# Folding a norm gain into the weight split, reordering the first loads, and starting the first product on half the tokens

## The reference

```python
def rms_norm(x, g):
    y = x * lax.rsqrt(jnp.mean(x * x, axis=-1, keepdims=True) + RMS_EPS)
    return y * g

h = rms_norm(x, norm1_g)          # x: (1, 512, 1024), norm1_g: (1024,)
proj = h @ w_in                   # w_in: (1024, 2816)
qa, ka, va, qb, kb, vb, gb = jnp.split(proj, ...)
...
```

## Time and profile before

| | us |
|---|---|
| time of the kernel before, median of 3 runs (601.34 to 603.32) | 601.63 |
| time of the profiled execution | 602.76 |
| its span in the profile | 601.0 |
| TensorE busy | 570.4 (95%) |
| VectorE busy | 422.0 (70%) |
| ScalarE busy | 350.4 (58%) |
| GpSimd busy | 133.9 (22%) |
| first pass of a product (block 0) starts at | 24.42 |
| last pass of block 0 hands over to block 1 at | 35.33 |

### The profile page before, as it was taken

One profiled execution on the slowest core, in us unless ns is written; L12 is line 12 of the kernel. 1 busy time (PEld: TensorE's weight loads), 2 busy tenths in 40 slices (PEclk: granted clock), 3 DMA queues, 4 the chain that ended last, 5 costly groups with the idle time before them and its releaser, 6 DMA issues.

```text
span 601.0 us, 8110 instructions
## 1 busy us (share of the span) xinstructions
PE 570.4 (95%) x2791; PEld 465.9 (78%) x2792; DVE 422.0 (70%) x559; ACT 350.4 (58%) x458; POOL 133.9 (22%) x116
## 2 busy tenths in 40 slices
PE   4899999999999999997999999999999999999973
PEld 3788878888877888876788888888888888888851
DVE  3812565554673854275489989889989889989867
ACT  4723435583133433340678778878778878778623
POOL 4320000000000000015503443233444233411170
PEclk9999999999999999998999999999999999999997
DMA  8996222202220236896399999999999999993163
GB/s 300 380 368 211 70 71 71 70 1 71 70 71 0 71 106 247 280 369 225 94 336 360 376 382 372 371 371 366 372 384 379 373 373 371 360 387 120 43 258 140
DMA packets 72141, 144.85 MB, mean 241 GB/s; under 512 B 3907, under 2 KB 13291, under 8 KB 71985
## 3 DMA queue, kind: packets, MB, share of 16 engines
q1 hardware_dynamic: 65936, 125.49, 59.1%
q0 software_dynamic: 6176, 19.00, 9.0%
HBM read 132.89 MB, written 14.71 MB: 246 GB/s over the span
## 4 chain that ended last, share of the span: by engine, by line
PE 83%; DVE 7%; DMA 4%; issue 2%; ACT 2%; SPq 1%; POOL 1%; POOLq 0%; DVEq 0%; ACTq 0%
PE ps L1226 23%; PE ps L1228 22%; PE ps L1227 22%; PE ps L1233 5%; DMA arena<-w_in 2%; PE ps L1298 2%; PE ps L1268 2%; PE ps L1241 2%; PE ps L1335 1%; PE ps L1323 1%; DMA arena<-y_dram 1%; PE ps L1289 1%; PE ps L1362 1%; DVE res L1187 1%; DVE act_lo L836 1%
## 5 line engine op out<-in xcount | busy, mean ns | idle before, releaser
L1026 DVE TENSOR_TENSOR lo_ring<-arena,hi_ring 128x2048 fp32r<-128x2048 f32 x94 | 215.2, 2292 | 37.6 <-ACT hi_ring L741 36.6
L1226 PE MATMUL ps<-hi_ring,act_hi 128*128 128x512 f32 x576 | 232.2, 403 | 1.2 <-DVE act_lo L836 1.2
L1228 PE MATMUL ps<-hi_ring,act_lo 128*128 128x512 f32 x576 | 225.2, 391 | 0.0
L1227 PE MATMUL ps<-lo_ring,act_hi 128*128 128x512 f32 x576 | 224.7, 390 | 0.0
L741 ACT ACTIVATE hi_ring<-arena 128x2048 fp32r<-128x2048 f32 x94 | 180.1, 1917 | 20.8 <-PE ps L1228 20.8
L1226 PEld LDWEIGHTS ps<-hi_ring,act_hi 128*128 128x128 f32 x576 | 108.4, 188 | 28.2 <-issue 6.0
L1228 PEld LDWEIGHTS ps<-hi_ring,act_lo 128*128 128x128 f32 x576 | 108.3, 188 | 23.6
L1227 PEld LDWEIGHTS ps<-lo_ring,act_hi 128*128 128x128 f32 x576 | 108.5, 188 | 20.5
L827 DVE TENSOR_TENSOR lo_ring<-arena,hi_ring 128x512 fp32r<-128x512 f32 x68 | 45.0, 688 | 43.3 <-ACT hi_ring L615 42.8
L539 POOL DMA_INDIRECT y_dram<-y,row_info x15 | 16.1, 1072 | 154.8 <-issue 154.8
L836 DVE TENSOR_TENSOR act_lo<-ps,act_hi 128x512 fp32r<-128x512 f32 x64 | 41.6, 683 | 11.0 <-ACT act_hi L779 4.9
(11 more groups left out here) (179 smaller groups left out, 546.7 us busy)
## 6 DMA issues: line engine op xcount, KB each, us to landing
arena<-w_gate SPq DMA_DIRECT2D x32, 1024.0 KB, 11.9
arena<-w_up SPq DMA_DIRECT2D x32, 1024.0 KB, 11.7
arena<-w_down SPq DMA_DIRECT2D x32, 1024.0 KB, 12.0
arena<-w_in SPq DMA_DIRECT2D x16, 512.0 KB, 9.4
y_dram<-arena POOLq DMA_DIRECT2D x8, 512.0 KB, 11.2
arena<-w_out SPq DMA_DIRECT2D x4, 1024.0 KB, 5.1
arena<-y_dram SPq DMA_DIRECT2D x8, 512.0 KB, 6.8
arena<-w_in SPq DMA_DIRECT2D x3, 1024.0 KB, 15.8
```

The lines of the kernel that those rows point to most:

```text
L1026: nc.vector.tensor_tensor(lo(N1 + n12), raw(n12), hi(N1 + n12).bitcast(F32), ALU.subtract).then_inc(lo_done, 1)
L1226: nc.tensor.matmul(dst, a_hi, b_hi, start=start, stop=False)
L1227: nc.tensor.matmul(dst, a_hi, b_lo, start=False, stop=False)
L1228: return nc.tensor.matmul(dst, a_lo, b_hi, start=False, stop=stop)
```

## The change

It has four parts.

1. **The gain.** `norm1` only multiplies x by the reciprocal root, with a TENSOR_SCALAR. The gain comes as 8 columns of 128 values (`gain1_col`, in the buffer `over`), fetched by GpSimd's first DMA in runs of one 4-byte element. In the split of blocks 0 to 10 ScalarE's copy has the gain column as its scale, and VectorE's subtraction becomes a SCALAR_TENSOR_TENSOR (raw times gain minus high). For blocks 0 and 1 that is two instructions for each piece on VectorE, for block 2 two on both engines, for blocks 3 to 10 one.
2. **The loads.** SyncE issues x 0, the identity alone (64 KB), x 1, weight block 0, x 2, x 3, weight block 1, the rest of `keep`, and then blocks 2 to 14. GpSimd issues five of its loads only when x 3 has landed.
3. **The start.** There are four `h_buf`, and tile t has bank 4+t for its transposes: first for its first four blocks of 128 (half 0), later, when the low part of these is written, for the other four (half 1). Block 0 is multiplied in two passes over the tokens: tiles 0 and 1 (256 columns), then tiles 2 and 3. The squares go to SBUF (`hi_ring`) instead of PSUM. The fills are 2, 10 and 10.
4. **The order.** ScalarE and VectorE mix the splits of block 0 into the work on the tiles; the splits of blocks 1 and 2 come behind all of it. `STEPS` starts with block 1.

```diff
-START_FILL = (2, 4, 6, 2, 12)
+START_FILL = (2, 10, 10)
...
-STEPS = [(g, t) for g in range(N1 - 2) for t in range(T)] + [(g, t) for t in range(T) for g in (N1 - 2, N1 - 1)]
+STEPS = [(g, t) for g in range(1, N1 - 2) for t in range(T)] + [(g, t) for t in range(T) for g in (N1 - 2, N1 - 1)]
...
-        h_buf = [region(O_P, D), region(O_PT, D)]
-        gain1 = region(O_QKB, D)
+        h_buf = [region(o, D) for o in (O_P, O_PT, O_QKB, O_QKB + D)]
+        gain1_col = over[:, T * N_LOGITS:T * N_LOGITS + KD].bitcast(F32)
...
+            load_x(0)
+            sp.dma_start(ident, table[:, C_IDENT:C_IDENT + P]).then_inc(ident_in, 16)
+            load_x(1)
+            load1(0)
+            load_x(2)
+            load_x(3)
+            load1(1)
+            sp.dma_start(keep[:, P:C_KEEP], table[:, P:C_KEEP]).then_inc(keep_in, 16)
+            for g in range(2, N1):
                 load1(g)
...
+            pool.dma_start(gain1_col, bass.AP(norm1_g.tensor, 0, [[1, P], [P, KD]]), allow_slow_non_contiguous=True
+                           ).then_inc(gain1_in, 16)
...
+            pool.wait_ge(x_in[T - 1], 16)
+            pool.dma_start(sinks[:, :], bass.AP(attn_sinks.tensor, 0, [[0, P], [1, 8]])).then_inc(sinks_in, 16)
...
             pool.wait_ge(rel_copied, 1)
...
-                nc.scalar.activation(dst, src, ACT.Copy).then_inc(hi_done, 1)
+                for cols, gain in gains(g, piece):
+                    if gain is None:
+                        ins = nc.scalar.activation(dst, src, ACT.Copy)
+                    elif g == 2:
+                        ins = nc.scalar.activation(dst[:, cols], src[:, cols], ACT.Copy, scale=gain)
+                    else:
+                        ins = nc.scalar.activation(dst, src, ACT.Copy, scale=gain)
+                ins.then_inc(hi_done, 1)
...
+            square_x(0)
+            square_x(1)
+            turned_hi(0, 0)
+            split_piece(0, 0)
+            turned_hi(1, 0)
+            split_piece(0, 1)
+            square_x(2)
+            square_x(3)
+            split_piece(0, 2)
+            turned_hi(2, 0)
+            split_piece(0, 3)
+            turned_hi(3, 0)
             for t in range(T):
+                turned_hi(t, 1)
             for piece in range(4):
                 split_piece(1, piece)
+            for piece in range(4):
+                split_piece(2, piece)
...
-                nc.vector.tensor_tensor(dst, src, src_hi.bitcast(F32), ALU.subtract).then_inc(lo_done, 1)
...
+                    elif g < 2:
+                        for a in range(2):
+                            ins = nc.vector.scalar_tensor_tensor(dst[:, :, a, :], src[:, :, a, :], gain,
+                                                                 src_hi[:, :, a, :].bitcast(F32), ALU.mult, ALU.subtract)
+                    else:
+                        ins = nc.vector.scalar_tensor_tensor(dst, src, gain, src_hi.bitcast(F32), ALU.mult, ALU.subtract)
...
-                nc.vector.scalar_tensor_tensor(h_buf[t % 2], res_t[:, t, :], rms[:, t:t + 1], gain1,
-                                               ALU.mult, ALU.mult).then_inc(h_ready, 1)
+                nc.vector.tensor_scalar(h_buf[t], res_t[:, t, :], rms[:, t:t + 1], None, ALU.mult).then_inc(h_ready, 1)
...
+            def first_block(half, k):
+                tok = slice(half * 2 * P, (half + 1) * 2 * P)
+                w_hi, w_lo = (as_chunks(v)[:, k, :] for v in (hi(0), lo(0)))
+                pe.wait_ge(lo_done, k + 1)
+                for t in range(T):
+                    cols = slice(t * P, (t + 1) * P)
+                    ins = triple(ps[:, t, tok], w_hi[:, cols], w_lo[:, cols], ht_hi[:, k, tok], ht_lo[:, k, tok],
+                                 half == 0 and k == 0, False)
+                    if half and k == 3:
+                        ins.then_inc(mm_done, 1)
...
+            fill(START_FILL[0])
+            turn_h(0, 0)
+            fill(START_FILL[1])
+            turn_h(1, 0)
...
+            fill(START_FILL[2])
+            pe.wait_ge(h_lo, 2)
+            first_block(0, 0)
+            first_block(0, 1)
...
+            turn_h(2, 0)
+            turn_h(3, 0)
+            first_block(0, 2)
+            first_block(0, 3)
+            turn_h(0, 1)
+            turn_h(1, 1)
+            pe.wait_ge(h_lo, T)
+            first_block(1, 0)
+            first_block(1, 1)
+            turn_h(2, 1)
+            turn_h(3, 1)
+            first_block(1, 2)
+            first_block(1, 3)
```

123 lines of the change are left out of this document (65 added, 58 removed).

## The result

The changed kernel takes 596.04 us (median of 4 runs, 593.51 to 596.89); the kernel before, on the same chip, 602.25 (601.34 to 603.32). The ratio is 0.9889, with a 95% interval of 0.9854 to 0.9925: 1.1% faster. The forecast was 597.1, in a range of 595.0 to 600.2, and faster by more than 0.3%.

What follows compares the result with a forecast made beforehand. TensorE bounds the kernel; its start on block 1 counts: 15.7 + 11.5 + 3.0 + 0.4 + 0.2 = 30.8 against 35.33, 4.5 us gained off the 601.63 median, giving 597.1, range 595.0 to 600.2.

Steps and rivals of the forecast that it cites:

- Loads: SyncE's queue at the start: in the new order x 1 ends at 6.7 us, block 0 at 11.2, x 3 at 15.6.
- The line read off the old queue: SyncE's bytes moved against time in the kernel before, used to place the new loads; called late bounds.
- First pass: TensorE's first 256-column pass of block 0, behind half tiles, fills and bias product: at 15.7 us (14.5 to 16.6).
- Block 0: TensorE's 96 passes at 0.12 (11.5 us), six half tiles (3.0), a wait (0.4) and slower first passes (0.2).
- the half width at full price: Rival in block 0: 256-column passes take as long as 512, 21.8 us instead of 11.5; time 607.4, chance 0.07.
- The wait for piece 3: In block 0, TensorE comes at 21.1 but piece 3 is split at 21.4: 0.4 us of waiting.
- The six half tiles: Transposes on TensorE between block 0's passes: six at 0.5 us, 3.0 in all.
- Block 1: Starts at 30.8; VectorE gives pieces from 30.0 to 32.5, TensorE asks from 30.8 to 32.9: fits by a few tenths.
- After that: Behind blocks 1 and 2: later ring slots, position bias and split costs cost nothing, so the 4.5 us reach the end.
- The start stays slow: Rival: TensorE stays at 1.2 GHz through all fills, or a load is late; first pass 18 to 20, 600.6, chance 0.09.

Runs made afterwards that it cites:

- Experiments 4: The changed kernel with two fills in each of the three places instead of 2, 10 and 10: 597.26 us, ratio 0.9916 to the kernel before.
- 5: The changed kernel with four fills instead of ten before block 0's first pass (2, 10, 4): 595.86 us, ratio 0.9891 to the kernel before.
- kernels 1: The changed kernel with the old order of loads on SyncE and GpSimd: 603.25 us, ratio 1.0013 to the kernel before.
- 3: The changed kernel with block 0 in one pass of 512 tokens, second-half transposes nearly where they were: 605.84 us, ratio 1.0067 to the kernel before.
- 8: The changed kernel with block 0 in one pass of 512 tokens, all second-half transposes between pieces 1 and 2: 601.15 us, ratio 0.9989 to the kernel before.

## Why the prediction was right, and where it was off

**Loads.** x 1 was expected at 6.7 and came at 7.75; block 0 at 11.2, and came at 11.15. The line read off the old queue held for 2 MB and was 1 us short for the tile, at no cost. The constants' identity came at 4.64 (expected 5.0).

**First pass, 15.7 forecast, 14.73 measured.** This is the term that was mis-sized. `norm1` was taken at the old instruction's 1.285 us and took 0.75, so that the first half tile was turned by 7.85 and not by 8.3. The estimate from the Trainium skill's table ("VectorE: DVE Perf Modes", section "The perf-mode tier table"), in the sentence beside the sum, was 0.6, nearer than the row that I took. The clock was put to rise at 11.2 and rose at about 10.3, which gives another 0.4. Both lay within the stated 14.5 to 16.6. One reading in the sum was off: 0.24 for a pass at the low level is a group's busy time over its count, which includes the end of the last pass; from start to start it is 0.213, and in block 0 a half tile takes 0.4 and not 0.5. As said there, the fills and not the data held the queue, by 1.3 us (13.46 to 14.73). Experiments 4 and 5 don't show what that is worth: with fewer fills their data was written at 14.45 and 14.48.

**Block 0, 15.1 us forecast, 14.81 measured.** A pass of 256 columns takes 0.12, as taken, in each run of passes from 14.73 to 29.54. The rival of the half width at full price falls: the 96 weight loads take 0.19 each, 18 us if none of them were hidden, and they start every 0.12 us. With it falls the rule of the Trainium skill ("TensorE: Matmul & The Clock Gate", section "The mechanism") as it was quoted, that a load overlaps matmuls only in other rows of the array; the same section also speaks of a background weight buffer, which the prediction left out. The wait for piece 3 was put at 0.4. The waits of TensorE in the changed kernel, 4 to 30 us (us in total, times, longest):

```profile
PE ps L1299 <- DMA keep<-table: 4.6, 1, 4.6
PE ps L1286 <- DVE arena L897: 1.1, 1, 1.1
PE ps L1279 <- DVE lo_ring L875: 0.4, 1, 0.4
```

It is 0.4. The six half tiles took 0.4 each, not 0.5. On the other side, the first pass behind transposes or a wait took 0.2 instead of 0.12, five times, 0.4 us where 0.2 had been added. So two small misses of opposite sign partly cancel in this term.

**Block 1.** It fits by a few tenths, said the forecast; from its first pass to the landmark it took 11.22 us against 11.08 before. **After that**, nothing was to be lost, and 0.09 us were. Between 29.5 and 75 us no engine but GpSimd (in its chain for the position bias) waited for a transfer, so blocks 5 and 6 and the masks came in time, as forecast.

**Not foreseen.** Block 1 ended 5.7 us earlier instead of 4.5, which taken off 601.63 gives 595.9. The profile's other 1.26 us come from the memset: it began 7.0 us earlier where VectorE's instruction began 5.7 earlier, and so was over in time. It looks like chance rather than an effect of the shift: over the ten traces in which the memset was left alone it starts anywhere from 1.9 us before the instruction to 0.3 after it, and the 1.41 us of the kernel before is the longest of all. I had read no row of that stretch. Whether any of these 1.26 us are in the median is not shown. *The start stays slow*, a rival with a chance of 0.09, did not occur with this kernel, but kernels 1, 3 and 8 show it: first passes at 19.65 to 20.40 and at 1.2 GHz.

## What to carry to other kernels

A first product that can begin on half of its operand and a load order that brings its weights early are worth little or nothing apart and 5.7 us together; cost such edits jointly, and undo them one at a time. A stall at the start of a matrix chain costs its own length and then, in kernels 1, 3 and 8, 1.4 to 2.4 us of lower clock; filler passes in front of the first product cost nothing here and bring up to 1.1 us. Compare two traces only beyond their scatter, which is 1 us at this start and 2.4 us around the gathers; kernels that repeat a start unchanged tell it. When the difference of two traces holds a piece that the change doesn't touch, look at that piece in all traces before counting it as a gain.
